# Row layout of the expert weights and the order of the router chain in a fused two-block transformer kernel

## The reference

```
for l in range(2):
    ...
    h = mem_xattn(x, mem, wq_x[l], wk_x[l], wv_x[l], wo_x[l])
    x = layer_norm(DN_ALPHA * x + h, ln_g[l, 1], ln_b[l, 1])
    h = grouped_moe(x, w_router, b_router, w_gate[l], w_up[l], w_down[l])
    x = layer_norm(DN_ALPHA * x + h, ln_g[l, 2], ln_b[l, 2])

def grouped_moe(x, w_router, b_router, w_gate, w_up, w_down):
    scores = softmax(xt @ w_router + b_router)          # 16 experts, 4 groups of 4
    # the group with the largest sum of its top-2 scores; its top-2 experts; renormalised gates
    ...
    for e in range(16):
        h = jax.nn.silu(xt @ w_gate[e]) * (xt @ w_up[e])  # w_gate, w_up: 1024 x 512
        y = y + gate[:, e:e + 1] * (h @ w_down[e])        # w_down: 512 x 1024
```

## Time and profile before

| | |
|---|---|
| median of three runs | 2280.56 us (2277.51 to 2281.64) |
| time of the profiled execution | 2278.92 us |
| its span, first to last instruction | 2277.1 us |
| busy: PE, PEld, DVE, ACT, GpSimd | 98%, 84%, 71%, 57%, 3% |
| mean granted clock of PE | 0.990 |
| moved by DMA | 490.93 MB, mean 216 GB/s |
| expert stages of the second block | about 1490 to 1760 us and 1980 to 2260 us |

### The profile page before, as it was taken

One profiled execution on the slowest core, in us unless ns is written; L12 is line 12 of the kernel. 1 busy time (PEld: TensorE's weight loads), 2 busy tenths in 40 slices (PEclk: granted clock), 3 DMA queues, 4 the chain that ended last, 5 costly groups with the idle time before them and its releaser, 6 DMA issues.

```text
span 2277.1 us, 31229 instructions
## 1 busy us (share of the span) xinstructions
PE 2220.8 (98%) x13248; PEld 1916.0 (84%) x13248; DVE 1612.7 (71%) x1577; ACT 1286.8 (57%) x1360; POOL 57.9 (3%) x71
## 2 busy tenths in 40 slices
PE   8999999999999999999999999999999999799997
PEld 7888989788888889897888998887777998687775
DVE  6765855777477557466774666589999666689997
ACT  5434644554344446445543544578887555488885
POOL 1000100000000001000000000000000000100000
PEclk9999999999999999999999999999999999899999
DMA  7755443455555554434664555479998554399995
GB/s 243 218 186 169 148 139 126 163 186 187 193 174 185 188 180 134 152 129 164 199 191 168 181 185 185 141 283 384 385 382 330 181 185 167 131 338 383 388 374 198
DMA packets 309952, 490.93 MB, mean 216 GB/s; under 512 B 15504, under 2 KB 205120, under 8 KB 309808
## 3 DMA queue, kind: packets, MB, share of 16 engines
q1 hardware_dynamic: 305712, 475.35, 61.2%
q0 software_dynamic: 3104, 10.38, 1.6%
q10 hardware_dynamic: 992, 3.15, 0.4%
HBM read 487.40 MB, written 1.44 MB: 215 GB/s over the span
## 4 chain that ended last, share of the span: by engine, by line
PE 78%; DVE 10%; DMA 7%; ACT 3%; issue 2%; DVEq 0%; SPq 0%; ACTq 0%
PE PS L807 14%; PE PS L734 14%; PE PS L730 14%; PE PS L731 13%; PE PS L810 7%; DVE RL L2203 5%; DMA RINGS<-w_down 4%; DMA RINGS<-w_gate 3%; PE PS L1422 2%; ACT RH L1662 2%; PE PS L1419 2%; PE PS L1042 1%; PE PS L1007 1%; PE PS L981 1%; PE PS L992 1%
## 5 line engine op out<-in xcount | busy, mean ns | idle before, releaser
L2203 DVE TENSOR_TENSOR RL<-RINGS,RH 128x2048 fp32r<-128x2048 f32 x448 | 1011.3, 2272 | 421.5 <-ACT RH L1662 419.5
L1662 ACT ACTIVATE RH<-RINGS 128x2048 fp32r<-128x2048 f32 x447 | 848.6, 1900 | 453.2 <-PE PS L734 375.3
L807 PE MATMUL PS<-HTS,RH 128*128 128x512 f32 x1384 | 416.3, 397 | 1.2 <-DVE HTS L2189 1.2
L730 PE MATMUL PS<-RH,HTS 128*128 128x256 f32 (+1 forms) x1184 | 342.2, 305 | 0.4 <-DVE HTS L2185 0.4
L731 PE MATMUL PS<-RH,HTS 128*128 128x256 f32 (+1 forms) x1184 | 336.1, 300 | 0.0
L807 PEld LDWEIGHTS PS<-HTS,RH 128*128 128x128 f32 x1384 | 249.7, 189 | 48.7 <-issue 1.6
L810 PE MATMUL PS<-HTS,RL 128*128 128x256 f32 x1408 | 283.3, 281 | 0.0
L734 PE MATMUL PS<-RL,HTS 128*128 128x256 f32 (+1 forms) x1184 | 261.5, 299 | 0.0
L810 PEld LDWEIGHTS PS<-HTS,RL 128*128 128x128 f32 x1408 | 228.9, 188 | 15.2
L730 PEld LDWEIGHTS PS<-RH,HTS 128*128 128x128 f32 x1184 | 223.8, 189 | 11.9 <-issue 2.5
L731 PEld LDWEIGHTS PS<-RH,HTS 128*128 128x128 f32 x1184 | 224.7, 190 | 7.2
(11 more groups left out here) (463 smaller groups left out, 2969.3 us busy)
## 6 DMA issues: line engine op xcount, KB each, us to landing
RINGS<-w_in SPq DMA_DIRECT2D x64, 1024.0 KB, 5.3
RINGS<-w_gate SPq DMA_DIRECT2D x64, 1024.0 KB, 9.3
RINGS<-w_up SPq DMA_DIRECT2D x64, 1024.0 KB, 9.4
RINGS<-w_down SPq DMA_DIRECT2D x64, 1024.0 KB, 9.1
RINGS<-ffn_w_up SPq DMA_DIRECT2D x44, 1024.0 KB, 5.3
RINGS<-ffn_w_down SPq DMA_DIRECT2D x44, 1024.0 KB, 4.9
RINGS<-ffn_w_gate SPq DMA_DIRECT2D x43, 1024.0 KB, 5.4
RINGS<-w_out SPq DMA_DIRECT2D x16, 1024.0 KB, 4.9
```

Of the source, the lines that this page charges most:

```text
L730: mm(dst, a_[0], b_[0], start=start, stop=False)
L807: return mm(PS[:, bank + c, :], wh[:, k, c * P:(c + 1) * P], HTS[:, :, k, :], start=(k == 0), stop=(k == K - 1))
L1662: A(splits.buffer(RH, RH3)[:, 0:width], RINGS[:, slot, 0:width], ACT.Copy).then_inc(wh_ready, 1)
L2203: TTn(RL[:, slot, 0:width], RINGS[:, slot, 0:width], splits.buffer(RH, RH3)[:, 0:width].bitcast(F32), ALU.subtract).then_inc(wl_ready, 1)
```

## The change

1. **Rows of the loads.** Chunks of w_gate, w_up and w_down are loaded with neighbouring rows on one partition: partition p holds rows 4p to 4p+3 (w_gate, w_up) or 2p and 2p+1 (w_down), 8 KB in one piece. The router's weights are loaded likewise, four rows of 64 bytes in one piece of 256.
2. **Features in that order.** The operands that meet these weights take their features in the same order: the transposes of X for the router and the gather pick every fourth float (`by_four`), the transposes of the hidden rows and the selection every second (`by_two`).
3. **XL on DVE.** The remainders of X are made by DVE (`rows_rest`) in place of GpSimd.
4. **Order in the router chain.** DVE makes row tile 0's remainder before the router's arithmetic and tile 1's before PLACE; in layer 1 the split that stood ahead of the arithmetic comes later. ACT rounds the second tile before it copies the router's sums.
5. **Late tables.** The gates come after DVE's first split behind the branch; SEATG and the other SEATX (now `seat_tables` on DVE too) come after its second split in expert 0. PE's `seat_tables` moves from the end of expert 0 to expert 1, behind its first chunk, and ACT's `seats` with it.
6. **Idle products.** In layer 1 PE makes 3 products of 512 columns of constants ahead of the transposes, 3 behind the router's product and 1 behind the positions; nobody reads them.

```diff
...
-                src_r = a["w_router_2"].rearrange("(k p) n -> p k n", p=P)
-                load(src_r, lambda r: r[:, 0:K * NE].rearrange("p (k n) -> p k n", n=NE))
+                src_r = a["w_router_2"].rearrange("(i p k) n -> p i (k n)", p=P, k=4)
+                load(src_r, lambda r: r[:, 0:K * NE].rearrange("p (i n) -> p i n", i=2))
...
                 def downs(e):
-                    many(2, lambda j: rows(a["w_down_2"][l], e, j * 256))
+                    for j in range(2):
+                        load(a["w_down_2"][l, e, j * 256:(j + 1) * 256, :].rearrange("(p k) n -> p (k n)", p=P), lambda r: r)
 
                 ring.experts = ring.n
                 for e in range(NE):
                     for n in ("w_gate_2", "w_up_2"):
                         for i in range(2):
-                            src = a[n][l, e, i * 512:(i + 1) * 512, :].rearrange("(k p) n -> p k n", p=P)
-                            load(src, lambda r: r.rearrange("p (k n) -> p k n", n=DE))
+                            load(a[n][l, e, i * 512:(i + 1) * 512, :].rearrange("(p k) n -> p (k n)", p=P), lambda r: r)
                     if e:
                         downs(e - 1)
...
-                    if k == 2:
-                        for t in range(T):
-                            pool.wait_ge(xh_ready, T * l + t + 1)
-                            nc.gpsimd.tensor_tensor(XL[t], X[:, t, :], XH[:, t, :].bitcast(F32), ALU.subtract).then_inc(xl_ready, 1)
...
+            def in_order(k):
+
+                return slice(k * P, (k + 1) * P)
+
+            def by_four(k):
+
+                return slice(k // 4 * 512 + k % 4, (k // 4 + 1) * 512, 4)
+
+            def by_two(k):
+
+                return slice(k // 2 * S + k % 2, (k // 2 + 1) * S, 2)
...
                     for k in range(2):
-                        nc.tensor.transpose(PS[:, bank + b, k * S:k * S + P], src[:, 0, (2 * b + k) * P:(2 * b + k + 1) * P], IDENT)
+                        nc.tensor.transpose(PS[:, bank + b, k * S:k * S + P], src[:, 0, block(2 * b + k)], IDENT)
...
-            def transpose_x(n, v, upper=None, bank=0):
-
-                transpose_halves(X, n, x_rows, 2 * v + 1, (x_left, v + 1), 1, upper, bank)
+            def transpose_x(n, v, upper=None, bank=0, block=in_order):
+
+                transpose_halves(X, n, x_rows, 2 * v + 1, (x_left, v + 1), 1, upper, bank, block)
...
+                def idle_products(bank, count):
+
+                    for _ in range(count):
+                        mm(PS[:, bank, :], IDENT, CON[:, O_MB:O_MB + 512], start=True, stop=True)
+
                 splits.enter()
                 if l == 0:
                     unit_ahead(11, 2)
+                else:
+                    idle_products(3, 3)
                 n = tr2(l, 3)
-                transpose_x(n, version(1, l, 2), taken_at(1, 11)[1] if l == 0 else None)
+                transpose_x(n, version(1, l, 2), taken_at(1, 11)[1] if l == 0 else None, block=by_four)
                 slot = ring.next()
                 splits.n += 1
...
+                else:
+                    idle_products(5, 3)
...
                             at = (k * tiles + t) * P
-                            last = nc.tensor.transpose(PS[:, 2 + at // 512, at % 512:at % 512 + P], EHID[:, t, k * P:(k + 1) * P], IDENT)
+                            last = nc.tensor.transpose(PS[:, 2 + at // 512, at % 512:at % 512 + P], EHID[:, t, by_two(k)], IDENT)
...
                     for k in range(4):
-                        last = mm(PS[:, bank, k * P:(k + 1) * P], EHID[main_rows(e), 0, k * P:(k + 1) * P], SEL[main_rows(e), e // 2, :], start=True, stop=True)
+                        last = mm(PS[:, bank, k * P:(k + 1) * P], EHID[main_rows(e), 0, by_two(k)], SEL[main_rows(e), e // 2, :], start=True, stop=True)
...
+                else:
+                    idle_products(5, 1)
...
                         for k in (2 * b, 2 * b + 1):
-                            dst, at = PS[:, GBANK[b], (k % 2) * S:(k % 2 + 1) * S], slice(k * P, (k + 1) * P)
+                            dst, at = PS[:, GBANK[b], (k % 2) * S:(k % 2 + 1) * S], by_four(k)
...
+                        if e == 1:
+                            seat_tables()
...
-                        if e == 0:
-                            seat_tables()
-                        else:
+                        if e:
...
                 rows_rounded(0)
                 ht_copy(tr2(l, 3), HT)
-                split(back=3)
+                rows_rounded(1)
                 chunk()
                 A(RLT, PS[0:2 * NE, 4, 0:S], ACT.Copy).then_inc(rt_cols, 1)
                 A(EPS[:, 1:2], EPS[:, 0:1], ACT.Exp)
                 act.wait_ge(rt_in, l + 1)
                 A(SMALL[:, 256:288], SMALL[:, 256:288], ACT.Exp).then_inc(rt_exp, 1)
-                rows_rounded(1)
+                split(back=3)
                 if l == 0:
...
+                        if e == 1:
+                            seats()
...
                         if e == 0:
-                            seats()
...
-                    split()
-
+
+                def rows_rest(t):
+                    dve.wait_ge(xh_ready, T * l + t + 1)
+                    TTn(XL[t], X[:, t, :], XH[:, t, :].bitcast(F32), ALU.subtract).then_inc(xl_ready, 1)
+
+                rows_rest(0)
                 ring.n += 1
...
-                            spread(SMALL[:, 468 + 4 * t:472 + 4 * t], 2, 4), ALU.mult)
+                        last = TTn(GATE[:, :, t].rearrange("p (g i) -> p g i", i=4), SMALL[:, 416 + 16 * t:432 + 16 * t].rearrange("p (g i) -> p g i", i=4),
+                                   spread(SMALL[:, 468 + 4 * t:472 + 4 * t], 2, 4), ALU.mult)
+                    link(last)
...
+                rows_rest(1)
                 dve.wait_ge(oh_ready, l + 1)
...
                 TSc(CROWDED, SMALL[:, 500:501], SEATS + 0.5, None, ALU.is_gt).then_inc(crowd_known, 1)
-                gates()
-                for t in range(T):
-                    TTn(SEATG[:, :, t, :], spread(CON[:, O_NTH:O_NTH + P], 1, NG_), spread(PLACE[:, t, 0:NG_], 2, P), ALU.is_equal)
-                for g in range(1, NG_):
-                    last = expert_seats(g)
-                last.then_inc(seat_ready, 1)
                 wait_apart(dve, crowd_known, l + 1, consts_loaded, 16 * NLOAD)
                 crowded = dve.value_load(CROWDED[0:1, 0:1], min_val=0, max_val=1)
...
+                        if e == 0:
+                            seat_tables()
...
+                    def seat_tables():
+
+                        for t in range(T):
+                            TTn(SEATG[:, :, t, :], spread(CON[:, O_NTH:O_NTH + P], 1, NG_), spread(PLACE[:, t, 0:NG_], 2, P), ALU.is_equal)
+                        for g in range(1, NG_):
+                            last = expert_seats(g)
+                        last.then_inc(seat_ready, 1)
+
+                    split()
+                    gates()
                     gathered(0)
+                    split()
                     for e in range(NE):
...
-                    sparse, paired = steps.n - apart, NE + T
+                    sparse, paired = steps.n - apart, NE + T + 3
...
-                    dve.wait_ge(seat_ready, 2 * l + 2)
-                    if l == 0:
-                        split()
+                    gates()
+                    dve.sem_inc(seat_ready, 1)
+                    split()
...
```

More of the change, by code:

```diff
@@ L883, in transpose_rows, with transpose_halves @@
                     last.then_inc(tr_ready, 1)
-            def transpose_halves(src, n, rows, first, left=None, tail=1, upper=None, bank=0):
+            def in_order(k):
[4 more added lines that the diff above has]
+                return slice(k // 2 * S + k % 2, (k // 2 + 1) * S, 2)
+            def transpose_halves(src, n, rows, first, left=None, tail=1, upper=None, bank=0, block=in_order):
                 pe.wait_ge(ht_l, n * 4 + 4)
@@ L901, in transpose_halves @@
                     for k in range(2):
-                        last = nc.tensor.transpose(PS[:, bank + b, k * S + P:(k + 1) * S], src[:, 1, (2 * b + k) * P:(2 * b + k + 1) * P], IDENT)
+                        last = nc.tensor.transpose(PS[:, bank + b, k * S + P:(k + 1) * S], src[:, 1, block(2 * b + k)], IDENT)
                     last.then_inc(tr_ready, 1)
-            def transpose_x(n, v, upper=None, bank=0):
-                transpose_halves(X, n, x_rows, 2 * v + 1, (x_left, v + 1), 1, upper, bank)
+            def transpose_x(n, v, upper=None, bank=0, block=in_order):
+                transpose_halves(X, n, x_rows, 2 * v + 1, (x_left, v + 1), 1, upper, bank, block)
             def transpose_y(n, made, bank=0):
@@ L2853, in gates @@
                     for t in range(T):
-                        TTn(GATE[:, :, t].rearrange("p (g i) -> p g i", i=4), SMALL[:, 416 + 16 * t:432 + 16 * t].rearrange("p (g i) -> p g i", i=4),
-                            spread(SMALL[:, 468 + 4 * t:472 + 4 * t], 2, 4), ALU.mult)
```

(3 more changed lines are left out.)

## The result

The changed kernel takes 2293.92 us (median of 4, 2292.09 to 2295.48), the one before 2279.03 (4 runs, 2277.41 to 2281.64): a ratio of 1.0069, 95% interval 1.0057 to 1.0081. It is 14.9 us slower, where 16 to 17 us faster were forecast and the range ended at 2287. The profiled execution has a span of 2290.3 us, 13.2 more than before.

A forecast was written before the change was run, and what follows sets the result against it. Transfers were taken to set the pace of the expert groups, just above PE and DVE. Loads -15.4, layer 0's router +0.5, layer 1's -2.0 sum to -16.9: span 2277.1 to 2260.2, median 2263.7, forecast 2264; range 2253 to 2287.

The forecast's parts named there:

- the feature order at nothing: X transposes, gather and selection: picking features with a step costs no time; free if stepping adds up to 13 ns a load.
- DVE's stepped write: Comparison writing every fourth float, 1.7 ns an element against 1.1; supports the rival of slower gather loads, 2286, chance 0.17.
- 22 us for the gathers: Slow-load rival: products every 0.21 us, +18 in six gathers inside the stages, about +4 in two in router chains; chance 0.17.
- The selection's step of two: Selection product's weight load, every second float: taken at no cost; if it paid too, 19 us more, 2305.
- +0.5 and -2.0: Router chains up to the first selection: layer 0 +0.5 us (-0.4 to +1.3), layer 1 -2.0 (-3.0 to +0.5).
- DVE's queue: DVE's work from router to first selection: branch, chunks, gates, remainders, tables, ending at 1507.3 in layer 0, 1996.5 in layer 1.
- the start of expert 0: Layer 1: gather from 1977.5, then branch 1.2, chunk 2.2, gates 0.7, remainders 1.25; start near 1983.3, was 1989.22.
- 7.8 was taken: PE's table products ahead of layer 0's first selection: taken at 7.8 us, ending at 1516.0.
- PE waiting some 3 us for DVE: Expert 1's first chunk: a new wait of about 3 us that gives back expert 0's earlier start.
- 310.6 forecast: Expert weight loads: time in ns of one 8 KB packet, giving 422 GB/s.
- the 20.7: Time lost in both expert stages, first to last selection, against PE's floor: 9.2 + 11.5 us; 22.0 with the last experts.
- 70% taken: Share of the 22.0 us lost in the expert stages that faster loads bring back: -15.4 us; bounds 25% to 100%.

The follow-up runs named there:

- experiment 1: Changed kernel, but the gather takes 128 neighbouring features again (wrong feature order, same amount of work): 2267.9 us against 2278.17 for the kernel before.
- experiment 12: Changed kernel with steps of 1, 2, 8 and 4 floats in a layer's four gathers: one execution, 2279.19 us.
- experiment 6: Changed kernel with XH and XL written in the weights' order, gather plain; only PE's table products and ACT's copies early again: 2268.03 us against 2277.88 before.
- experiment 5: Changed kernel with XH and XL written in the weights' order, gather plain, and the late tables undone: 2262.07 us against 2277.88 for the kernel before.
- 13: Changed kernel with only the late tables undone, gather still stepped: 2282.65 us against 2278.72 for the kernel before.
- experiment 11: Changed kernel with all loads and features in the old order and the tables early: 2274.46 us against 2278.69 for the kernel before.
- experiment 3: Changed kernel with all loads and features in the old order, router chain and late tables as changed: 2279.07 us against 2278.17 for the kernel before.

## Why the prediction was wrong

**The step that failed: the feature order at nothing.** The prediction took nothing for the 16-byte step "since the product's moving side is read at 118/256 = 0.46 ns a column, so a load at 0.82 uses half of what PE can draw". The step brought the load from 188 to 330 ns, and a product of the gather to 0.235 us. Experiment 1 shows the price: 26.0 us. Of this 12 + 11 lie in the six gathers inside the stages. The other two make expert 0 start 3.7 and 2.0 us later behind the start of the gather, but in these two executions the way from there to the first selection is 1.1 and 3.1 shorter than in experiment 1 (26.0 for 27.0 and 27.1 for 30.2), mostly by the clock of the table products in layer 1 (8.9 us for 12.0), which is no merit of the step. The argument took its 0.46 ns from columns at neighbouring addresses; experiment 12 shows that it does not carry over to columns 16 bytes apart. The row that pointed the right way was there: DVE's stepped write, 1.6 times. It was put at 0.17 as a rival, at 2286: its 22 us for the gathers were 24 to 26 (a product every 0.235 us, where it had 0.21), and the rest of the way to 2293.9 is the second step below. The selection's step of two cost 5 ns a load, as forecast nothing. The sentence of the Trainium skill (SBUF — State Buffer, The DMA port swizzle) that spoke against the change, a penalty for each access that crosses to a new line, was right in both cases: 142 ns more for the step of four floats, 5 for the step of two.

**The second, smaller one: the late tables.** Forecast was +0.5 and -2.0. Without the slow gather (experiment 1 against before) the first selection of layer 0 comes 1521.39 - 1518.46 = 2.9 later; and in layer 1 the way from the last selection of layer 0 grows from 250.85 to 253.54, +2.7. Both routers together are 7.1 off. The sum had DVE's queue right: layer 1's gather starts 4.0 earlier (217.8 us behind that selection, 221.8 before; forecast 3.9), L2835 is at 0.18 us, the clock in that gather is 1.00. (Its terms for the start of expert 0 make 1982.9, not 1983.3; nothing hangs on it.) What it lacked is what the tables had covered. PE's products at the end of expert 0 lay over ACT's load of the silu table and its first silu; without them PE waits 0.45 + 1.40 us for ACT, and the products then run at a lower clock: 8.9 and 12.0 us in experiment 1, where 7.8 was taken. All profiled executions together show it as a tendency. These products take 6.3 to 6.4 us where the granted clock is 0.98 or more, and 12.0 to 12.2 where it is 0.50. With the tables early they take 6.3 to 8.4 (mean 7.3 of 16 stages, those of the kernel before among them), with the tables late 8.6 to 9.0 nine times and 12.0 three times (mean 9.7; experiment 6, late in part, is left out). "PE waiting some 3 us for DVE" was 0.82 + 0.45 in layer 0. Experiments 5 and 13 show the price of the late tables: 8.3 and 11.3 us, experiment 11 4.6; PE's products early and DVE's tables late (experiment 6) give back only 2.3.

**What was right.** The transfers were the bound and the runs of 8 KB loosen it: 308 ns a packet (310.6 forecast), 426 GB/s (422). The Trainium skill's 3 cycles a packet (DMA: Bandwidth & Descriptors, Why small descriptors are slow), from which the prediction estimated 399 GB/s, do not agree with it. Experiment 1 has groups of 63.5 us (63 to 64), and from selection 0 to selection 14 220.05 and 219.95 us where before had 225.8 and 228.1: 13.9 of the 20.7 come back, 67% (70% taken); with the last experts it is 16.7 us (15.4 forecast). DVE's stall in GpSimd's shadow is gone.

**The sum anew**, in the spans: stages -16.7; router and tables +2.9 and +2.7; that makes -11.1, and experiment 1 has 2266.1 - 2277.1 = -11.0. The step adds 2290.3 - 2266.1 = 24.2: +13.2.

**What stays open.** Why the late tables cost 4.6 with the old loads, 6 to 8 with the new and 11 with the stepped gather. Part may be that a late start fills the ring where transfers are the bound; no run separates it from the clock of the table products, which differs between executions (in layer 0 12.0 us in the profile of experiment 3 and 8.9 in that of experiment 1, with the same instructions). That ACT's silu wait is what lets the clock fall was not tried by itself; the same waits stand ahead of products of 8.6 us and of 12.0.

## What to carry to other kernels

A layout that makes a transfer's runs longer puts a step into whoever reads the matching operand. Look for the reader that has the fewest instructions to pay with, and choose the shortest run that gives the gain: here 4 KB with a step of two (2266.6 and 2260.5 us), not 8 KB with a step of four (2293.9 and 2282.7). Before work is moved off the end of a stage, list what waits it covers on its own engine, another engine's first use of a function included, and price the moved products at either clock.

## What the runs showed that was not expected

A step of 16 bytes costs time on every engine that met it, GpSimd least: PE's load of 128 columns of float32r from 188 to 330 ns, ACT's copy of 1024 from 1.06 to 2.08 us, DVE's subtraction from 1.22 to 2.03, GpSimd's from 2.42 to 2.90 only. A step of 8 bytes costs PE 3 to 5 ns. PE's 32 products of two columns take 3.7 us in layer 0 of experiment 5, at a granted clock of 0.98 over the table products, and 6.9 in experiment 6, at 0.50, behind a wait of 1.8 us.
